# A four-layer hybrid encoder on Trainium2: RWKV bonus products moved into the chunk loop, attention scores moved ahead of the last gate tiles, mLSTM spreads mixed with query and key tiles

## What is computed

```python
# RWKV-7, 16 heads of 64, after the recurrence gave y
y = head_norm(y, ln_g, ln_b, RW_GN_EPS)
y = y + jnp.sum(r * k * r_k, axis=-1, keepdims=True) * v      # the bonus
y = y.reshape(B, T, RW_WIDTH) * silu(g)
return y @ w_out
# attention, chunks of 64 that see themselves and the chunk before; q, k with partial rope
s = einsum('bcqhgd,bckhd->bhgcqk', qc, kb) * (SW_HEAD ** -0.5)
m = maximum(max(s, -1), sink)
p = exp(s - m); p = p / (sum(p, -1) + exp(sink - m))
o = einsum('bhgcqk,bckhd->bcqhgd', p, vb) * silu(g)
# mLSTM, 4 heads: c = silu(conv(u)); q = c @ w_q; k = c @ w_k / sqrt(128)
P = exp(D - m_t) * einsum('bcthd,bcjhd->bctjh', q, k)          # weights from the gates' rows
y = (head_norm(hm) + skip * c) * silu(z)
```

## Time and profile before

| | us |
|---|---|
| median of 3 runs | 1402.02 (1401.89 to 1403.1) |
| the profiled execution, its own time | 1403.4 |
| its span, first to last instruction | 1401.6 |
| PE busy | 1333.7 (95%) |
| PE weight loads busy | 696.0 |
| DVE / ACT / POOL busy | 716.1 / 430.7 / 97.4 |
| mean granted clock of TensorE | 0.990 of 2.4 GHz |

### The profile page before, as it was taken

How to read it: one execution, slowest core, us unless ns; L and a number is a source line. 1 busy time by engine, 2 the same in 40 slices (tenths; PEclk the granted TensorE clock), 3 DMA queues, 4 the chain that set the end, 5 groups by cost and what they waited for, 6 DMA issues and landing times. The chain is left out here.

```text
span 1401.6 us, 23655 instructions
## 1 busy us (share of the span) xinstructions
PE 1333.7 (95%) x10169; PEld 696.0 (50%) x10169; DVE 716.1 (51%) x1394; ACT 430.7 (31%) x1020; POOL 97.4 (7%) x118
## 2 busy tenths in 40 slices
PE   5999999999999999889999998999999999999998
PEld 3444454488544444564444445544443444468743
DVE  5686776955631011361244013532676875976653
ACT  3114364045211020551212052512121366125401
POOL 0000252011100000000000000000000044010010
PEclk9999999999999999999999988999999999999999
DMA  6221222100600222101322221021522222200321
GB/s 218 76 75 49 72 69 68 30 4 5 243 0 18 79 82 77 46 4 58 90 62 75 75 61 30 31 60 54 165 75 62 58 65 73 60 2 5 115 86 60
DMA packets 111760, 92.46 MB, mean 66 GB/s; under 512 B 5084, under 2 KB 99588, under 8 KB 111144
## 3 DMA queue, kind: packets, MB, share of 16 engines
q1 hardware_dynamic: 110952, 88.82, 20.8%
q10 hardware_dynamic: 704, 2.13, 0.4%
HBM read 84.65 MB, written 6.29 MB: 65 GB/s over the span
## 5 line engine op out<-in xcount | busy, mean ns | idle before, releaser
L1072 PE MATMUL bank<-arena 128*128 128x512 f32 x960 | 420.3, 595 | 1.5 <-ACT arena L650 1.5
L1020 PE MATMUL bank<-arena 64*64 64x64 f32 (+6 forms) x6848 | 313.7, 246 | 17.9 <-issue 10.3
L1072 PEld LDWEIGHTS bank<-arena 128*128 128x128 f32 x960 | 179.9, 190 | 227.8 <-issue 216.3
L1020 PEld LDWEIGHTS bank<-arena 64*64 64x64 f32 (+3 forms) x6848 | 202.0, 133 | 136.6 <-issue 121.6
L168 ACT ACTIVATE arena<-arena 128x512 f32<-128x512 f32 x40 | 25.1, 630 | 218.0 <-DVE arena L1003 110.7
L778 DVE SCALAR_TENSOR_TENSOR arena<-arena 128x512 f32<-128x512 f32 x96 | 73.3, 809 | 0.0
L1776 PE MATMUL bank<-arena 128*128 128x512 f32 x160 | 69.2, 593 | 0.6 <-PEq L342 0.6
L676 ACT ACTIVATE arena<-arena 32x128 f32<-32x128 f32 x128 | 54.4, 425 | 37.0 <-DVE arena L800 34.2
L591 POOL MEMSET arena<- 128x8 f32 x2 | 0.2, 111 | 898.5 <-DVE arena L931 898.5
L2185 PE MATMUL bank<-arena 128*128 128x512 f32 x128 | 56.2, 593 | 0.9 <-DVE arena L2233 0.9
L351 PE MATMUL bank<-arena 128*128 128x512 f32 x128 | 55.5, 593 | 1.0 <-PEq L1521 1.0
(11 more groups left out here) (228 smaller groups left out, 1533.0 us busy)
## 6 DMA issues: line engine op xcount, KB each, us to landing
arena<-in_rw_w_in SPq DMA_DIRECT2D x66, 512.0 KB, 4.1
arena<-in_ml_w_in SPq DMA_DIRECT2D x24, 512.0 KB, 3.9
arena<-in_sw_w_in SPq DMA_DIRECT2D x20, 512.0 KB, 3.9
arena<-in_rw_w_out SPq DMA_DIRECT2D x16, 512.0 KB, 7.4
spill<-arena SPq DMA_DIRECT2D x2, 2048.0 KB, 9.4
arena<-spill SPq DMA_DIRECT2D x2, 2048.0 KB, 14.0
arena<-in_sw_w_out SPq DMA_DIRECT2D x8, 512.0 KB, 3.6
arena<-in_ml_w_out SPq DMA_DIRECT2D x8, 512.0 KB, 3.6
```

Source lines behind the costliest of these rows:

```text
L1020: mm = lambda out, a, b, start=True, stop=True: nc.tensor.matmul(out, a, b, start=start, stop=stop, skip_group_check=True)
L1072: last = nc.tensor.matmul(bank[:, :], slot[:, k, :], mix_at[what][:, k, :], start=k == 0, stop=k == KT - 1)
```

## The change

**RWKV.** `bonus(c)` follows `outputs(c)` for each of the eight chunks, all in bank 1, each waiting until DVE has used the one before. DVE's `times_values(c)` follows `complete_u(c+1)` in the loop and writes into R; the last one comes after `finish(0)`. ACT's three copies and POOL's three products are gone. To free bank 1, `turn_bk` of chunks 1 to 6 uses banks 0 and 2, and its second half waits for the masked `products_r` and for x. The first spread pass has three tiles (banks 4, 5, 0), the rest follow the output products of k = 1, 3, 5 (3 and 4; 5 and 6; 7). 16 idle transposes instead of 18. The final norm's weights are loaded into V's place once bonus 7 is used.

**Attention.** One block, `sw_layer`. PE: gate tiles 0 to 3, transposes 0 to 3, gate tile 4, transposes 4 to 7, gate tile 5, transposes 8 and 9, scores 0 and 1, gate tiles 6 and 7, then the chunk loop. The 20 idle transposes ahead of the loop are gone, those of the last two chunks stay. ACT and DVE do chunk 0 and 1's exponentials and normalisations ahead of the last two gate tiles' sigmoids and products.

**mLSTM.** The list's end becomes cols, then mu and q alternating by head, then init and k alternating by head. The product with skip moves from DVE at the end of `ml_project` to POOL in `ml_chunks` (eight tensor-tensor operations of 128 x 512 with a broadcast column).

```diff
-RW_OUT_BANKS = ((1, 2, 3, 7), (0, 4, 5, 6))
+RW_OUT_BANKS = ((2, 3, 6, 7), (4, 5, 0, 1))
-    t_bank = lambda c, q: m.bank[q if c else 6 + q]
+    t_bank = lambda c, q: m.bank[2 * q if c else 6 + q]
...
+                    if c > 0 and q == 1:
+                        pe.wait_ge(gr_evac.handle, gr_evac.at(2 * c + 1))
+                        pe.wait_ge(xs_ready.handle, xs_ready.at(c + 1))
...
                 if c + 1 < NC:
                     products_r(c + 1)
-                else:
-                    bonus(0)
-                    bonus(1)
                 outputs(c)
+                bonus(c)
...
-            bonus(2)
             sums(1, SUMMED, T)
-            for j in range(3, KT):
-                bonus(j)
-            spread(range(4))
-            pe.wait_ge(bonus_kept.handle, bonus_kept.at(1))
-            m.run_idle(out_bank(0, 0), 18)
+            spread(range(3))
+            m.run_idle(out_bank(0, 0), 16)
...
-                if k in (1, 3):
-                    spread(range(k + 3, k + 5))
+                if k in (1, 3, 5):
+                    spread(range(k + 2, min(k + 4, KT)))
...
                     advance(c)
                     complete_u(c + 1)
+                    times_values(c)
...
             for j in range(KT):
                 finish(j)
+                if j == 0:
+                    times_values(KT - 1)
```

```diff
+            for j in range(4):
+                gate_tile(j)
+            for n in range(4):
+                turn_qk(n)
+            gate_tile(4)
+            for n in range(4, 8):
+                turn_qk(n)
+            gate_tile(5)
+            turn_qk(8)
+            turn_qk(9)
+            scores(0)
+            scores(1)
+            gate_tile(6)
+            gate_tile(7)
...
+            keep_qk(8)
+            keep_qk(9)
+            exps(0)
+            exps(1)
+            sigmoid(6)
+            sigmoid(7)
+            evac(0)
...
+            maxima(0)
+            maxima(1)
+            normalise(0)
+            normalise(1)
+            gate_by_sigmoid(6)
+            gate_by_sigmoid(7)
+            maxima(2)
...
-            m.run_idle(m.bank[4], 20)
```

```diff
-    tiles += [("cols", 0)] + [("mu", h) for h in range(ML_H)]
-    tiles += [(w, h) for w in "qk" for h in range(ML_H)] + [("init", h) for h in range(ML_H)]
+    tiles += [("cols", 0)] + [(w, h) for h in range(ML_H) for w in ("mu", "q")]
+    tiles += [(w, h) for h in range(ML_H) for w in ("init", "k")]
...
-            for j in range(KT):
-                nc.vector.tensor_scalar(cc[:, j, :], cc[:, j, :], col(ML_SKIP, j), None, ALU.mult)
...
+        @block.gpsimd
+        def _(pool):
+            for j in range(KT):
+                nc.gpsimd.tensor_tensor(cc[:, j, :], cc[:, j, :], m.view(A_PT + P + ML_SKIP + j, 1).to_broadcast([P, T]), ALU.mult)
```

More of the change, by code:

```diff
@@ L1365, with sw_layer @@
 SW_KV = 4
-def sw_project(m, sinks, n0):
+def sw_layer(m, sinks, n0):
     nc = m.nc
@@ L1398, in _, with gate_tile @@
         def _(pe):
-            w = n0
+            def gate_tile(j):
+                m.weights_arrived(pe, n0 + 12 + j)
+                slot = m.view(m.slot(n0 + 12 + j), KT, P)
+                if j < 4:
+                    pe.wait_ge(qkv_evac.handle, qkv_evac.at(4 + j + 1))
+                else:
+                    pe.wait_ge(g_used.handle, g_used.at(j - 3))
+                for k in range(KT):
+                    last = nc.tensor.matmul(m.bank[4 + j % 4][:, :], slot[:, k, :], xt[:, k, 1:T + 1], start=k == 0,
+                                            stop=k == KT - 1)
+                last.then_inc(g_done.handle, 1)
@@ new lines, in turn @@
+            def turn(c):
+                pe.wait_ge(normed.handle, normed.at(c + 1))
+                for q in range(2):
+                    if c >= 1:
+                        pe.wait_ge(p_evac.handle, p_evac.at(2 * c - 1 + q))
+                    else:
+                        pe.wait_ge(g_used.handle, g_used.at(5 + q))
+                    for k in range(4):
+                        last = nc.tensor.transpose(m.bank[4 + q][0:keys(c), P * k:P * k + P], prob[c % 2][:, 4 * q + k, 0:keys(c)],
+                                                   ident)
+                    last.then_inc(p_turned.handle, 1)
@@ new lines, in _ @@
+            for n in range(4):
[10 more added lines that the diff above has]
+            gate_tile(7)
+            for c in range(NC):
+                if c + 2 < NC:
+                    scores(c + 2)
+                turn(c)
+                if c >= NC - 2:
+                    m.run_idle(m.bank[0], 8)
+                if c >= 1:
+                    outputs(c - 1)
@@ new lines, in exps @@
+            def exps(c):
+                p, st = prob[c % 2], small[c % 2]
+                act.wait_ge(s_max.handle, s_max.at(c + 1))
+                if c >= 2:
+                    act.wait_ge(p_turned.handle, p_turned.at(2 * (c - 1)))
+                nc.scalar.activation(st[:, 2, :], st[:, 1, :], ACT.Exp)
+                for h in range(8):
+                    bank = m.bank[2 * (c % 2) + h % 2]
+                    last = nc.scalar.activation(p[:, h, 0:keys(c)], bank[:, P * (h // 2):P * (h // 2) + keys(c)], ACT.Exp,
+                                                bias=st[:, 0, h:h + 1], scale=C ** -0.5, accum_out=st[:, 3, h:h + 1])
+                last.then_inc(s_exp.handle, 1)
@@ L1453, in _, with evac @@
+            def evac(c):
+                for q in range(2):
+                    act.wait_ge(p_turned.handle, p_turned.at(2 * c + q + 1))
+                    if q == 0 and c >= 2:
+                        act.wait_ge(o_done.handle, o_done.at(c - 1))
+                    nc.scalar.activation(pt[c % 2][0:keys(c), 4 * q:4 * q + 4, :], m.bank[4 + q][0:keys(c), :], ACT.Copy)\
+                        .then_inc(p_evac.handle, 1)
             for n in range(8):
@@ L1639, in _ @@
[L1639 to L1648 removed]
+                normalise(c)
```

339 lines of the change are left out of this document (130 added, 209 removed).

## The result

The changed kernel takes **1391.95 us** in the median of 4 runs (1390.89 to 1394.1), the kernel before on the same chip 1401.95 (1398.76 to 1403.1): ratio 0.9934, 95% interval 0.9914 to 0.9955, so 10.0 us less where 4.0 were forecast, and below the range. Compared a second time, later on, it took 1393.98 (6 runs, 1390.81 to 1396.47) against 1400.67, just inside the range: ratio 0.9942, interval 0.9921 to 0.9963. By the mean of the two ratios the change brings 8.7 us.

A forecast was written before the change was run, and what follows sets the result against it. PE, busy for 95% of the span, was taken to bound the kernel. Terms -6.0 - 1.1 - 3.5 + 6.4 = -4.2, with 0.2 for POOL's company -4.0: 1398.0 us on the median, range 1393.5 to 1404.5.

The forecast's parts named there:

- (a): RWKV chunk loop: seven bonuses moved in at 1.0 us of PE each, 7.0 us more a layer, bounds 2 and 7.4.
- gaps close: Rival, RWKV loops: PE's issue gaps are waits for instructions that a bonus fills, up to 5 us a layer; chance 0.13.
- mLSTM order and skip: mLSTM up to the chunks: full clock and earlier barrier 6.0 us less, transposes behind it 1.1 less.
- Attention: From the end of the gate tiles to `turn(3)`: 20.2 us instead of 23.7, 3.5 less, bounds 2 and 4.5.
- quiet stretches: Rival: clock falls where PE now idles in RWKV tails and ahead of attention's `scores(4)`, 3.4 us a fall; chance 0.25.
- The RWKV tail: From the loop's end to the first output product: output products start at 370.3 instead of 375.35, 5.05 us less a layer.
- third pass: RWKV output products: three spread passes instead of two between products, 1.25 us more a layer.
- own signs of error: Wrong if PEclk shows 0.50 between 440 and 1395, period grows under 0.6 us, or PE awaits DVE in output products.

The follow-up runs named there:

- the doubled bonus: The changed kernel with each of the seven bonuses in the loop computed twice in a row: 1404.56 us, ratio 1.0027.
- the four-spread run: The changed kernel with the four mu spreads ahead of the four q tiles again, init and k still mixed: 1394.76 us, ratio 0.9945.
- the run with that part alone: The kernel before with the RWKV edits alone: 1401.24 us against 1401.48, ratio 1.0005.
- its run: The kernel before with the mLSTM edits alone (order of the tiles, skip products on POOL): 1396.89 us, ratio 0.9972.

## Why the prediction was wrong

**The step that failed** is (a), the price of the seven bonuses in the loop: "7 x 1.0 = 7.0 us more", with the reason "I take the upper part, since only gaps shortly behind `outputs` would shrink". The bonus is 0.91 us of PE in a chunk without a gap, so the price of one was right. But a layer's loop grew by 0.9 and 3.5 us in the traces shown, by 3.5 in the mean (149.2 less 142.2, halved): 7.0 us for two layers where 14.0 were forecast. That is the rival "gaps close", which had a chance of 0.13, at 3.5 of its 5 us a layer. Per chunk, the six with `turn_bk` stood 0.98 us above a chunk without a gap before (mean 10.18; the changed kernel's shortest 10.11 less the bonus makes 9.20) and stand 0.72 above it after (10.83 less 10.11). The seventh, which I had priced like the rest, became 0.4 shorter with a bonus in it (10.03 to 9.60 in the means). Part of the distance to the forecast is luck: 1393.98, the second median, lay inside the range.

Why, as far as the traces carry it: every gap ends 2.1 to 3.0 us after a transfer starts, as if PE lived till then on the instructions that it holds. Small products use these up fast; a chunk issues some 700 instructions in 9.4 us, a bonus four in 0.96. A bonus within those 2.5 us lets them pass, wherever the gap would have come. The traces count it so (PE's transfers in both loops that start 3 us or more before the loop's end): in the eleven profiles of the new loop 3 of the 120 transfers with a bonus begun in the 2.6 us behind them had a gap, and 107 of the 281 others; with the old loop 66 of 143. With the doubled bonus it is 0 of 14 and 7 of 22, so the gaps that are left stand behind transfers that no bonus meets, which fits the second one's full price. I looked at which products the gaps stood ahead of, and should have looked at when they end: the transfers were in the trace of before, and every gap ended about the same time behind one. The Trainium skill ("Runtime: NRT & Kernel Launch", "Instruction fetch mechanics") says that the sequencer fetches blocks of 16 KiB while it executes and that crossing a block is mostly hidden; the traces agree with the size and the fetching ahead, and with "mostly" for large products, but in these loops it is not hidden: the issue row has 7.6 to 10.3 us before the change, about 5 of 71 us a loop. Up to 7.6 a loop if all that the periods stand above a chunk without a gap is counted: six times 0.98 us and, by the same working, 1.7 in the seventh chunk (10.03 in the mean, the new shortest 9.24 less the bonus makes 8.33). That is an estimate, as no old chunk was so short: the shortest took 9.27 and, of the seventh, 9.34.

**The range** was wrong by its own rule. The text gave 2 to 7.4 a layer, so the low end had to reach 10 us under the forecast, to 1388; I took half of one rival, and 1391.95 lay outside.

**Everything else**, point by point. mLSTM order and skip: 7.1 forecast, 7.3 in the trace, 6.8 against the mean of four old profiles; mixing keeps the clock up (the four-spread run shows it), and the barrier without DVE is worth what it was priced at. What the Trainium skill says, that the clock follows how busy PE has been ("TensorE: Matmul & The Clock Gate", "What's actually happening"), doesn't tell these apart: PE is busy for all of the stretch in the rows of both orders, at 1.00 in one and 0.50 in the other. Attention: without a fall 3.66 (99.46 less 95.80), forecast 3.5; falls take back 0 to 1.7 of it, not the 3.4 of the rival "quiet stretches". The likely reason is that PE waits for DVE once a chunk there anyway. The RWKV tail: 5.08 and 5.39, forecast 5.05; third pass 1.25 and 1.29, forecast 1.25. The quiet-stretch rival was right about the places, and more often than its 0.25 said: the clock fell in attention in all eleven profiles, and in a little over half of the tails, at 0.9 us, though in none of the four in the changed kernel's own two profiles. Summed by these means: -6.8 mLSTM, -2.9 attention (96.9 less 99.8), -10.5 tails, +2.5 passes, +7.0 loops, +1.0 falls in the tails, -9.7 together; the ratios say -8.7. The RWKV terms alone make 0.0, as the run with that part alone has it; the mLSTM's 6.8 is 2.9 more than its run gave. Of my own signs of error two came true: PEclk 0.50 between 440 and 1395, and in the first layer a period grown by 0.3.

The first profile pair flatters the change: 12.6 us between the spans, as the execution before was 1.4 above its median, that after 1.1 below.

## To carry to other kernels

Where PE's stream is thousands of small products, part of its time is instruction supply: look when the "issue" gaps end against the instruction transfers, and price long PE work put between them at less than its duration: here half of it for the first bonus of a chunk, all of it for a second right behind. Right ahead of the longest stretch of small products it closed nearly all gaps in two kernels, for 1 to 2 us that the runs can't tell from nothing. And compare stretches, not totals, when a kernel's loops differ by 3 us from one execution to the next; a bound that was worked out belongs in the range.

## Not expected of the hardware

- All 212 gaps end 2.1 to 3.0 us after the start of a 16 KB instruction transfer; with the bonus right ahead of the dense stretch two kernels had 3 and 2 of them in both loops, where those with the bonus behind the outputs had 7 to 14 and those without one in the loop 13 to 19.
- The clock fell around `turn(2)` in 11 of 11 profiles behind a wait of 1.85 us, and in none of 5 when 15 and 5 idle transposes filled the waits; in the RWKV tails 13 of 24 against 0 of 8 with eight more in a wait of 1.0 us. These eight cost nothing: 7.75 us from the loop's end to the spreads either way.
- 64 satisfied waits in PE's queue put off its first product by 3.2 to 4.1 us, 128 by 6.6 to 6.8: about 0.05 us each.
- A tensor-tensor product of 128 x 512 with a broadcast column on POOL took 1.04 us, as long as the RWKV layer's product of a tensor with itself (L611, 14 times). There the product by eight columns, each broadcast over 64 tokens, took 1.22 (L601, 16 times). Each took the same, to 0.01 us, however long DVE was busy beside it; what makes the difference isn't shown.
